# Splitting x without GpSimd, ada blocks alone in the queue, and one ada vector computed a layer later

## The reference

```
m = silu(c) @ w_ada + b_ada                      # six vectors of 1024: m[0] .. m[5]
h = rmsnorm(y, g_pre_mix) * (1 + m[1]) + m[0]
u = h @ w_in                                     # 1024 x 2560
cat = [differential attention | neighbourhood or dense attention | multi-scale pooling](u)
y = y + m[2] * rmsnorm(cat @ w_out, g_post_mix)
h = rmsnorm(y, g_pre_ffn) * (1 + m[4]) + m[3]
f = routed experts(h) + shared expert(h)         # 64 experts, 8 chosen per token by sigmoid scores
y = y + m[5] * rmsnorm(f, g_post_ffn)
```

## Time and profile before

| | |
|---|---|
| median of three runs | 1502.33 us |
| the profiled execution's own time | 1498.62 us |
| its span, first to last instruction | 1496.8 us |
| PE / DVE / ACT / POOL busy | 1386.2 / 457.0 / 339.5 / 81.6 us |
| share of the chain that ended last | PE 86%, DVE 4%, DMA 4%, ACT 3% |
| moved by DMA | 509.68 MB, mean 341 GB/s |
| mean granted clock of TensorE, 1 being 2.4 GHz | 0.962 |

### The profile page before, as it was taken

The page is one execution under the profiler, slowest core; times in us unless marked ns, Lnnn a source line. Parts: engine busy times, 40 slices in busy tenths (PEclk is TensorE's granted clock), DMA queues, the critical chain, the costliest instruction groups (busy, mean ns, idle before and its releaser), DMA issues.

```text
span 1496.8 us, 23839 instructions
## 1 busy us (share of the span) xinstructions
PE 1386.2 (93%) x9650; PEld 783.0 (52%) x9650; DVE 457.0 (31%) x982; ACT 339.5 (23%) x607; POOL 81.6 (5%) x97
## 2 busy tenths in 40 slices
PE   3797888999999999999979696999999999999996
PEld 1575654455454554545458574455454554545443
DVE  1534543222222222222263446322222222222223
ACT  1423451111111111111152354111111111111111
POOL 2011040000000000000020204000000000000000
PEclk7799979999999999999989897999999999999998
DMA  9589845999999999999657534799999999999991
GB/s 358 194 299 403 334 194 201 395 411 407 399 398 410 410 404 410 390 413 406 244 182 279 202 132 169 276 391 412 406 392 417 397 407 412 393 417 394 404 413 46
DMA packets 84831, 509.68 MB, mean 341 GB/s; under 512 B 4736, under 2 KB 4736, under 8 KB 33344
## 3 DMA queue, kind: packets, MB, share of 16 engines
q1 hardware_dynamic: 82960, 503.93, 84.1%
q0 software_dynamic: 1840, 5.31, 1.1%
HBM read 506.60 MB, written 2.62 MB: 340 GB/s over the span
## 4 chain that ended last, share of the span: by engine, by line
PE 86%; DVE 4%; DMA 4%; ACT 3%; issue 1%; POOL 1%; SPq 0%; POOLq 0%; ACTq 0%; DVEq 0%
PE PS L814 30%; PE PS L845 16%; PE PS L789 13%; PE PS L637 10%; PE PS L806 8%; DMA weights<-in_w_ada 2%; DMA weights<-in_w_out 2%; PE PS L833 1%; PE PS L758 1%; PE PS L659 1%; PE PS L778 1%; PE PS L738 1%; ACT weights_split L912 1%; DVE h L1121 1%; PE PS L796 1%
## 5 line engine op out<-in xcount | busy, mean ns | idle before, releaser
L814 PE MATMUL PS<-weights,gathered 128*64 128x512 f32 x2112 | 464.5, 592 | 0.0
L814 PEld LDWEIGHTS PS<-weights,gathered 128*64 128x64 f32 x2112 | 151.5, 137 | 301.9 <-issue 301.9
L845 PE MATMUL PS<-weights,hiddenT 128*64 128x512 f32 x1056 | 241.1, 598 | 0.0
L789 PEld LDWEIGHTS PS<-pick,x_parts 128*128 128x128 bf16 x3264 | 182.6, 98 | 54.7 <-issue 54.7
L789 PE MATMUL PS<-pick,x_parts 128*128 128x128 bf16 x3264 | 194.0, 219 | 0.0
L1377 DVE SCALAR_TENSOR_TENSOR hidden<-PS,slot_gate,silu 128x256 f32<-128x256 f32 x66 | 32.0, 485 | 410.5 <-ACT silu L1019 410.5
L1026 ACT ACTIVATE y_hi<-PS 128x512 fp32r<-128x512 f32 x132 | 78.9, 597 | 304.7 <-PE PS L845 304.7
L1387 DVE TENSOR_TENSOR y_lo<-PS,y_hi 128x512 fp32r<-128x512 f32 x132 | 91.3, 692 | 154.1 <-ACT y_hi L1026 154.1
L845 PEld LDWEIGHTS PS<-weights,hiddenT 128*64 128x64 f32 x1056 | 69.9, 136 | 114.5 <-issue 113.1
L637 PE MATMUL PS<-weights_split,hT_high 128*128 128x512 f32 x448 | 110.0, 401 | 14.7 <-ACT weights_split L912 8.9
L1019 ACT ACTIVATE silu<-PS 128x256 f32<-128x256 f32 x66 | 25.4, 384 | 429.7 <-PE PS L814 429.7
(11 more groups left out here) (227 smaller groups left out, 982.1 us busy)
## 6 DMA issues: line engine op xcount, KB each, us to landing
weights<-in_w_gate SPq DMA_DIRECT2D x66, 2048.0 KB, 9.8
weights<-in_w_up SPq DMA_DIRECT2D x66, 2048.0 KB, 14.2
weights<-in_w_down SPq DMA_DIRECT2D x66, 2048.0 KB, 11.1
weights<-in_w_ada SPq DMA_DIRECT2D x24, 2048.0 KB, 13.9
weights<-in_w_in SPq DMA_DIRECT2D x10, 2048.0 KB, 9.6
weights<-in_w_out SPq DMA_DIRECT2D x4, 2048.0 KB, 16.9
weights<-in_ws_gate SPq DMA_DIRECT2D x2, 1024.0 KB, 4.8
weights<-in_ws_up SPq DMA_DIRECT2D x2, 1024.0 KB, 6.9
```

The source lines that it names most:

```text
L789: last = mm(PS[:, 5 + half, j * P:(j + 1) * P], x3[:, g, part, jj, :], pick[:, u % 2, g, 0:P], start=(g, part) == (0, 0), stop=(g, part) = ...
L814: last = mm(PS[64 * e:64 * e + 64, 4, :].rearrange("p (a n) -> p a n", a=2), xgT[:, b, j, 64 * e:64 * e + 64], w[:, e, :, j, :], start=j = ...
L845: last = mm(PS[64 * e:64 * e + 64, bank, :], hidT[:, j, 64 * e:64 * e + 64], w[:, e, j, n * HALF:(n + 1) * HALF], start=j == 0, stop=j == ...
```

## The change

It does five things.

1. The four subtractions that GpSimd makes for the parts of x go to VectorE, behind its copies of hT and ahead of its work on the scores. ScalarE writes the first part of each group right after its copy of that group's hT, and the second parts before the sigmoid of the scores.
2. The two spare places at the head of each layer's list go. The first "in" block of layer 0 is in the fifth place of the ring, so SyncE issues it without a wait, in two halves with a semaphore each; the second waits until the last of the four ada blocks has landed. Layer 0's list has four spare places ahead of the shared expert's weights instead.
3. GpSimd's loads from the lambda rows on wait until the first "in" block has landed.
4. In layer 0 ScalarE makes the upper part of "in" 0 ahead of the rows of hT, half by half as they land. The lambda sums, exponential and values go into the "in" products (n = 2 and n = 4).
5. Ada vector 2 of layer 1 is computed in layer 1. In layer 0's attention the latent group has (1, 1) vectors in its slots, in layer 1's the context group has (2, 0).

```diff
-ADA_IN_ATTENTION = (((2, 1), (2, 1)), ((1, 0), (1, 0)))
+NEXT_LAYER = 2
+ADA_IN_ATTENTION = (((2, 1), (1, 1)), ((2, 0), (1, 0)))
...
-    out = [("ada", layer, i, a) for i in range(3 if layer else EARLY, ADA) for a in range(2)]
+    out = [("ada", layer, i, a) for i in range(NEXT_LAYER if layer else EARLY, ADA) for a in range(2)]
     if layer + 1 < DEPTH:
-        out += [("ada", layer + 1, i, a) for i in range(3) for a in range(2)]
+        out += [("ada", layer + 1, i, a) for i in range(NEXT_LAYER) for a in range(2)]
...
-    return first + [("spare", 0), ("spare", 1)] + split("in", 5) + ada[:n] + split("out", 2) + ada[n:] + [("shared_gu",), ("shared_dn",)]
+    late = [("spare", k) for k in range(0 if layer else 4)]
+    return first + split("in", 5) + ada[:n] + split("out", 2) + ada[n:] + late + [("shared_gu",), ("shared_dn",)]
...
+                    if l == 0 and what == ("in", 1):
+                        sp.wait_ge(block_in[LAST_EARLY], 16)
+                    if l == 0 and what == ("in", 0):
+                        half = dst.shape[1] // 2
+                        sp.dma_start(dst[:, 0:half].rearrange("p (j n) -> p j n", n=HALF), src[0][:, 0:KT // 2, :]).then_inc(first_half_in, 16)
+                        src = [src[0][:, KT // 2:, :]]
+                        dst = dst[:, half:]
...
             root(0)
+            pool.wait_ge(block_in[LAST_EARLY + 1], 16)
             pool.dma_start(lam4[:, :, :, :], io["diff_lambda"].partition_broadcast(P)).then_inc(lam_in, 16)
...
-                for g in range(NG):
-                    blocks = h[:, g, :].rearrange("t (p j) -> t j p", j=KT)
-                    pool.wait_ge(tr_mm, NG * (3 * l + 2) + g + 1)
-                    pool.wait_ge(x_hi, NG * l + g + 1)
-                    nc.gpsimd.tensor_tensor(blocks, blocks, x3[:, g, 0, :, :], ALU.subtract).then_inc(x_rest, 1)
-                for g in range(NG):
-                    blocks = h[:, g, :].rearrange("t (p j) -> t j p", j=KT)
-                    pool.wait_ge(x_mid, NG * l + g + 1)
-                    nc.gpsimd.tensor_tensor(x3[:, g, 2, :, :], blocks, x3[:, g, 1, :, :], ALU.subtract).then_inc(x3_ready, 1)
...
+                if (l, name, part) == (0, "in", 0):
+                    half = BLOCK // 2
+                    act.wait_ge(first_half_in, 16)
+                    run(hi[:, 0:half], w[:, 0:half], ACT.Copy)
+                    hi, w = hi[:, half:], w[:, half:]
                 act.wait_ge(block_in[ring_of(k)], 16 * loads_of(k))
                 run(hi, w, ACT.Copy).then_inc(w_high, 1)
...
-                if l == 0:
-                    act.wait_ge(lam_e_in, 1)
-                    run(nlam[:, :, 2:4], nlam[:, :, 2:4], ACT.Exp).then_inc(lam_e, 1)
-                if l:
-                    high_weights(l, "in", 0)
+                high_weights(l, "in", 0)
                 modulated_rows(l)
-                if l == 0:
-                    high_weights(l, "in", 0)
                 high_weights(l, "in", 1)
...
+                    if l == 0 and n == 2:
+                        act.wait_ge(lam_e_in, 1)
+                        run(nlam[:, :, 2:4], nlam[:, :, 2:4], ACT.Exp).then_inc(lam_e, 1)
...
-                rows_out(3 * l + 2)
                 act.wait_ge(kv_out, 64 * (l + 1))
                 for g in range(NG):
+                    rows_out(3 * l + 2, (g,))
                     run(x3[:, g, 0, :, :], h[:, g, :].rearrange("t (p j) -> t j p", j=KT), ACT.Copy).then_inc(x_hi, 1)
-
-                def middle(g):
-
+                for g in range(NG):
                     act.wait_ge(x_rest, NG * l + g + 1)
                     run(x3[:, g, 1, :, :], h[:, g, :].rearrange("t (p j) -> t j p", j=KT), ACT.Copy).then_inc(x_mid, 1)
-
                 act.wait_ge(rlog_mm, l + 1)
                 run(s_[:, :, :], PS[:, 7, 0:NG * N_EXP].rearrange("p (g e) -> p g e", g=NG), ACT.Sigmoid).then_inc(s_ready, 1)
-                for g in range(NG):
-                    middle(g)
...
+                    if l == 0 and n == 2:
+                        lambda_sums()
+                    if l == 0 and n == 4:
+                        lambda_values()
                     dve.wait_ge(u_mm, 10 * l + 2 * n + 2)
...
                 rows_out(3 * l + 2)
+                for g in range(NG):
+                    blocks = h[:, g, :].rearrange("t (p j) -> t j p", j=KT)
+                    dve.wait_ge(x_hi, NG * l + g + 1)
+                    v.tensor_tensor(blocks, blocks, x3[:, g, 0, :, :], ALU.subtract).then_inc(x_rest, 1)
+                for g in range(NG):
+                    blocks = h[:, g, :].rearrange("t (p j) -> t j p", j=KT)
+                    dve.wait_ge(x_mid, NG * l + g + 1)
+                    v.tensor_tensor(x3[:, g, 2, :, :], blocks, x3[:, g, 1, :, :], ALU.subtract).then_inc(x3_ready, 1)
```

40 lines of the change are left out of this document (22 added, 18 removed).

## The result

| | before | after |
|---|---|---|
| median of four runs each | 1502.05 us (1498.34 to 1503.56) | 1481.19 us (1477.38 to 1485.24) |
| ratio of after to before, 95% interval | | 0.9865 [0.9833, 0.9897] |
| the profiled execution's own time | 1498.62 us | 1481.51 us |
| its span | 1496.8 us | 1479.7 us |
| share of the chain that ended last, PE / DMA | 86% / 4% | 90% / 1% |

What follows compares the result with a forecast made beforehand. The expert loop is PE-bound and untouched, so gains ahead of it arrive whole. Terms 10.1 + 3.0 + 9.2 + 0 = 22.3 us give 1476.3 for the profiled execution, median 1480.0 us, range 1472 to 1487.

Steps and rivals of the forecast that it cites:

- D: Layer 1's attention, one ada vector more: 0 us, ends -1.7 and +1.7.
- A: Start: small loads wait and ScalarE copies the "in" block earlier; PE starts at 41.1 instead of 51.23, gaining 10.1 us.
- B: Layer 0's latent-group attention, one ada vector less and no w_out wait: 3.0 us gained, ends 0.2 and 7.0.
- rival (1): Layer 0's attention: PE keeps 2.4 GHz, B is 6, total 1477.0 us; chance 0.13.
- C: Routers of both layers: subtractions moved to VectorE end the collisions with GpSimd and PE's mask waits; 9.2 us gained together.
- ScalarE's row: Router: ScalarE's 2.04 us per strided copy of the same h, nearest to the 2.2 us taken per VectorE subtraction.
- the case to which it leaned: Router: the two subtractions writing with the stride cost 4.1 us each, nothing left of C, sum 13.1 us.
- two halves of the balance: Layer 1: vector's product could add 1.7 us to the path; busier PE keeping its clock could be worth 1.7.
- (2): Start: ada blocks don't land sooner, the queue being limited otherwise; A is 5.0, total 1485.1 us; chance 0.15.
- (3): Router: VectorE's strided subtractions give the collision's time back; C is 0, total 1489.2 us; chance 0.11.
- (4): Router: comparisons are slow of themselves, each layer loses the 0.95 us slip, total 1491.1 us; chance 0.02.
- (5): Router: slower than before, subtractions eat A and B too, needing 4.8 us an operation; chance 0.02.

Runs made afterwards that it cites:

- the control: The changed kernel itself, unaltered, run again beside two later experiments; 1480.86 us (1478.68 to 1481.25, five runs).
- the run with the rows first: Changed kernel with ScalarE making layer 0's rows of hT ahead of the first "in" block's upper part, as before; 1487.65 us.
- the six products: Changed kernel plus six unread PE products in the idle times of the latent group's attention, in both layers; 1473.07 us.
- small loads early: Changed kernel without the wait on GpSimd's small loads, which start at once beside the ada blocks; 1487.05 us.
- the readers beside the comparisons: Changed kernel plus two unused GpSimd subtractions per layer that read SBUF, placed beside VectorE's comparisons; 1489.99 us, one run.
- the start's gain: Changed kernel plus ten unread PE products in the waits of the start; cached keys' transposes 1.6 us earlier, whole kernel 1478.26 us.
- the run that had both: Changed kernel plus unread PE products in the start, both layers' latent groups, ahead of each router and at the layers' boundary; 1480.11 us.

## Why the prediction was right, point by point

**The total.** 1480.0 forecast, 1481.19 measured, 1480.86 in the control; the range 1472 to 1487 holds all nine runs of the two. A hit as close as this is in part luck. For the profiled execution I had forecast 1476.3, and the two of the changed kernel took 1481.51 and 1481.12: 17.1 and 17.5 us won, and not 22.3. The medians are 20.9 us apart, as the profile of before was one of its short executions, 3.7 us under its median, while the two of the changed kernel lie at theirs. The stretches of PE's clock that the sum leaves out (D below) differ by as much as that.

**A, the start: 10.1 forecast, 10.45 measured.** The steps hold one by one. Last ada block at 31.4: used from 30.89. First "in" block landed at 36.8: 36.27. ScalarE's copy through at 38.6: 38.20 by the trace. PE at 41.1: 40.78. Undoing the queue part costs 5.13 us at the block, against 5.1 by the share of queue 0. A loss of 0.3 on the way through the "in" products I hadn't counted. That ScalarE's order counts as well as the queue is shown by the run with the rows first, 4.05 us.

**B: 3.0 forecast, 3.16 measured,** 3.8 in the control's profile and 2.7 by putting the vector back. PE takes the scores 6.1 us sooner (133.26, with the 10.2 us of lead taken off), the second slot's vector starts 2.9 us sooner at 143.17 and takes 4.37 us, against the 3.0 and 4.6 of the sum. The clock did fall as in the earlier trace rows, the w_out wait is gone (ScalarE's first copy at 149.09 had none), and rival (1), which said that the clock would stay, was wrong for this kernel; the six products show that what it described is there to be had.

**C: 9.2 forecast, 9.46 measured** in the first profile (5.66 and 3.80; 5.5 and 3.7 forecast), 7.4 in the control's (4.3 and 3.1), so the term is good to some 2 us and no better. The waits for the mask are gone in both; what varies is PE's clock beside them. The strided subtraction was priced at 2.2 us and took 2.05, also where it writes with the stride: it is L1256, in place in h, that does so, and L1260, whose output lies in order, took 2.03 each. So ScalarE's row was the near one. The rule on 16-byte lines that the prediction takes from the Trainium skill (SBUF — State Buffer, Door 1: The DMA port swizzle) agrees with the trace in that the jumps cost something, 2.05 against the plain 1.23; the case to which it leaned, the writers paying twice, isn't there. The scores' first operation comes 7.81 us behind the start of the router's product, before 7.51: a slip of 0.3 where I had 0.95. It makes no difference, since PE binds.

**D: 0 forecast, 0 for the vector, but the term was too narrow.** The two halves of the balance are there, each smaller than priced: the vector's product costs 0.7 us where I had 1.7, and the clock that PE keeps behind it gives 0.7 back. What I left out is that layer 1's clock differs from one execution of the same program to the next, ahead of the vector and behind it: from the loop's end to the router it took 168.2 and 171.6 us in two executions of the changed kernel, against 165.9 in the one profile of before. In the first profile this is the whole difference between the 22.3 forecast and the 17.1 seen: 10.15 + 3.16 + 5.66 + 3.80 = 22.8, minus 5.7. The control's profile is 4.8 us short of the 22.3: layer 1 has 2.4 of it, C 1.8, and layer 0's context group, whose clock fell too, 1.3; B gave 0.8 more.

**The rivals.** (2), (3) and (4) are excluded by runs: small loads early, the routers' rows, the readers beside the comparisons. (5) needed 4.8 us an operation, the trace has 2.05.

## What to carry to other kernels

Price a chain of loads by the share that other queues take of the DMA engines in just that window; here it came out to 0.1 us. Keep GpSimd off SBUF while VectorE does short operations on the path: each of them can be held for up to a whole GpSimd instruction (2.71 and 0.94 us here), by reads if it has two SBUF inputs, and by memsets if it is a cast or a tensor_scalar. And compare stretches between two traces only after a look at the granted clock in each, and not at its mean alone: 19.7 and 22.3 us went with means of 0.82 and 0.81 here, low at the group's end in one and at its beginning in the other. A product without a reader in an idle time of PE can be worth more than the idle time itself (7.8 us for some 6.9 here, a part of it in stages for which the cause isn't shown), but only where PE would be waiting anyway, and one that lands behind the wait costs all of its length.

## What was not expected of the hardware

- Six unread products per layer, some 5.7 us of PE work each layer, made the kernel 7.8 us faster (1473.07 against 1480.86) and narrowed its runs to 1.5 us. It is the version that beats both kernels, 30.3 us under the one before (1503.32; ratio 0.9799).
- The same program's layer 1 took 171.6 and 168.2 us in two executions, with the same instructions in the same order; the windows show a mean granted clock of 0.81 and 1.00 in one stage, which took 22.3 and 19.7 us.
- Memsets of 0.95 us held up VectorE's one-input operations of 0.17 us, to 0.94.
- The highest mean clock (0.983) did not go with the shortest time: it was reached with products that stood in the way.

Left open: what decides at which moment the clock falls in layer 1, whether the router's product (7.06 us at a clock of 0.50 in every trace here) would be shorter at full clock, and whether the start's gain of 1.6 us adds to the six products' gain, since the run that had both also had the misplaced ones.
